# The depthwise convolution of a decoder layer on TensorE, with the shifted copies as the stationary operand

## What is computed

```python
def token_mixers(h, ctx_a, ctx_b, w_in, b_in, w_dw_a, b_dw_a, ln_conv_g, ln_conv_b, w_dw_b, w_o, b_o):
    z = h @ w_in + b_in                                    # (B, T, D_IN)
    a_val, a_gate, g_b, g_c, b_val = jnp.split(
        z, [D_A, 2 * D_A, 2 * D_A + D_B, 2 * D_A + 2 * D_B], axis=-1)
    # group A: Conformer conv module (GLU -> dwconv31 -> LN -> swish)
    u = a_val * jax.nn.sigmoid(a_gate)
    ua, new_ctx_a = causal_depthwise(ctx_a, u, w_dw_a)
    ua = jax.nn.silu(layer_norm(ua + b_dw_a, ln_conv_g, ln_conv_b))
    # group B: short gated conv  B * conv3(C * h)
    v = g_c * b_val
    vb, new_ctx_b = causal_depthwise(ctx_b, v, w_dw_b)
    ub = g_b * vb
    out = jnp.concatenate([ua, ub], axis=-1) @ w_o + b_o   # shared output projection
    return out, new_ctx_a, new_ctx_b

def trunk_layer(x, ...):
    x = layer_norm(ALPHA * x + 0.5 * swiglu(x, f1_wg, f1_wu, f1_wd), ln_f1_g, ln_f1_b)
    m, new_a, new_b = token_mixers(x, ctx_a, ctx_b, ...)
    x = layer_norm(ALPHA * x + m, ln_mix_g, ln_mix_b)
    x = layer_norm(ALPHA * x + 0.5 * swiglu(x, f2_wg, f2_wu, f2_wd), ln_f2_g, ln_f2_b)
```

## Time and profile before

| | us |
|---|---|
| median of 3 runs | 1200.44 (1195.74 to 1337.34) |
| the profiled execution | 1198.1 |
| its span, slowest core | 1196.4 |
| spans of the 8 cores | 1189.4 to 1196.4 |
| mean granted TensorE clock of the cores | 0.993 to 0.998 |
| TensorE busy | 1169.1 (98% of the span) |
| VectorE busy | 571.3 (48%) |
| ScalarE busy | 260.4 (22%) |
| GpSimd busy | 149.4 (12%) |

### The profile page before, as it was taken

One profiled execution on the slowest core, in us unless ns is written; L12 is line 12 of the kernel. 1 busy time (PEld: TensorE's weight loads), 2 busy tenths in 40 slices (PEclk: granted clock), 3 DMA queues, 4 the chain that ended last, 5 costly groups with the idle time before them and its releaser, 6 DMA issues.

```text
span 1196.4 us, 18592 instructions; the slowest of 8 cores (1189.4 to 1196.4 us)
## 1 busy us (share of the span) xinstructions
PE 1169.1 (98%) x6724; PEld 632.8 (53%) x6724; DVE 571.3 (48%) x874; ACT 260.4 (22%) x561; POOL 149.4 (12%) x212
## 2 busy tenths in 40 slices
PE   7999999999999999999999999999999999999997
PEld 5444444466666544455566544444444466666443
DVE  1122217742222387577888974557225532222475
ACT  1111110011111000349645432223100011111000
...
GB/s 157 134 152 174 176 107 150 115 120 177 77 71 73 45 126 137 139 128 119 128 162 164 138 157 140 157 128 108 197 107 121 88 147 80 74 71 36 36 126 88
DMA packets 78888, 144.43 MB, mean 121 GB/s; under 512 B 39872, under 2 KB 42304, under 8 KB 78784
## 3 DMA queue, kind: packets, MB, share of 16 engines
...
## 4 chain that ended last, share of the span: by engine, by line
PE 90%; DVE 5%; issue 2%; DMA 1%; ACT 1%; POOL 0%; DVEq 0%; SPq 0%; ACTq 0%; POOLq 0%
PE ps L591 59%; PE ps L575 28%; PE ps L860 1%; DMA sb_xT<-xpq 1%; PE ps L684 1%; DVE sb_xq L487 1%; DMA sb_xq<-xk 1%; DVE sb_stt L497 1%; DVE sb_RH L1022 0%; PE ps L878 0%; DVE sb_RW L954 0%; DVE sb_xq L521 0%; PE ps L561 0%; DVE sb_RW L933 0%; DVE sb_xq L491 0%
## 5 line engine op out<-in xcount | busy, mean ns | idle before, releaser
L591 PE MATMUL ps<-sb_xT,sb_ring 128*128 128x344 bf16 (+3 forms) x4384 | 770.1, 337 | 13.1 <-DMA sb_xT<-xpq 4.5
L591 PEld LDWEIGHTS ps<-sb_xT,sb_ring 128*128 128x128 bf16 x4384 | 428.3, 98 | 335.5 <-issue 17.9
L612 DVE TENSOR_TENSOR sb_RH<-sb_sg,ps 128x344 bf16<-128x344 f32 (+3 forms) x224 | 129.0, 576 | 453.6 <-ACT sb_sg L610 449.2
L575 PE MATMUL ps<-sb_RW,sb_RH 128*128 128x512 bf16 x1364 | 295.6, 379 | 0.6 <-DVE sb_xq L491 0.6
L610 ACT ACTIVATE sb_sg<-ps 128x344 f32<-128x344 f32 (+3 forms) x224 | 113.9, 508 | 618.5 <-PE ps L591 607.7
L575 PEld LDWEIGHTS ps<-sb_RW,sb_RH 128*128 128x128 bf16 x1364 | 133.2, 98 | 161.9 <-issue 1.9
L470 POOL TENSOR_TENSOR sb_mv<-sb_mv,sb_neghalf 128x1 f32<-128x1 f32 (+1 forms) x47 | 51.1, 1087 | 459.3 <-DVE sb_mv L468 459.3
L487 DVE SCALAR_TENSOR_TENSOR sb_xq<-sb_xq,ps 128x1024 f32<-128x1024 f32 (+1 forms) x50 | 60.8, 1217 | 88.2 <-PE ps L575 83.3
L406 POOL DMA_DIRECT2D sb_ring<-wgu x87 | 47.6, 548 | 410.0 <-PE ps L591 403.3
L528 DVE SCALAR_TENSOR_TENSOR sb_xq<-sb_xq,sb_mv,sb_lnb 128x1024 f32<-128x1024 f32 (+1 forms) x50 | 64.1, 1283 | 11.0 <-POOL sb_mv L470 6.2
L497 DVE BATCH_NORM_STATS2 sb_stt<-sb_xq 128x6 f32<-128x512 f32 (+1 forms) x100 | 64.1, 683 | 3.5
...
## 6 DMA issues: line engine op xcount, KB each, us to landing
...
```

What stands on the lines that cost most here:

```text
L575: ins = e.matmul(ps[:n, bank(yb + h)], lhsT=lhs(f), rhs=rhs(f, h), start=(f == 0), stop=(f == nk - 1))
L591: ins = e.matmul(out, lhsT=ring[:, slot, cw:cw + 128], rhs=xT_rhs(b, k, tok0, n), start=(k == 0), stop=(k == KC - 1))
L612: P.op("dve", lambda e: e.tensor_tensor(out=hT[:, f, tok0:tok0 + n], in0=sg[:, p_ % 2, :n], in1=ps[:, bu * 512: bu * 512 + n], op=ALU.mult ...
```

## The change

- **Convolution.** Stationary and moving operand change places: R2, shifted by 0 to 4 columns, is loaded, and the wide weights move. The result has tokens in the partitions at once. The biased copy, accP and the float32 transposes (`out`, `flip`) are gone; `put` reads the convolution's own bank one item later.
- **Bias.** Ahead of each group of five, one matmul with three rows adds the bias: `ones` (3 x 128) against `brow`, three bf16 rows whose sum is the float32 bias. `use_consts` makes them: a load into slot 4 of xq, five VectorE operations on one partition, three transfers.
- **Weights of the convolution.** They have four slots in place of three (the room of accP). The lists that say where they are made are new: in block 0 all eight by VectorE pieces.
- **Places and banks.** Block 0 convolves in banks 4 and 5, block 1 in 6 and 7. In block 1 the convolutions and the output projection's tiles stand at other items. The last gating item of block 0 goes to banks 4 and 5.
- **Turns.** For block 1, the TensorE turn stands ahead of the output projection's tile, and its ScalarE copy behind the item's `out`.
- **Chunks.** The second FFN's block 0 begins with three chunks on its first 512 tokens, not two (`u_items(0, 3)`).

```diff
@@ the constants @@
+            P.op("dve", lambda e: e.memset(ones[:], 1.0), writes=["ones"])
+            lo, hi = xq[0:1, 4, 0:DA], xq[0:1, 4, DA:2 * DA]
+            P.op("sp", lambda e: e.dma_start(out=lo, in_=bcd), writes=[("xq", 4)], dma="xq4")
+            P.op("dve", lambda e: e.tensor_copy(out=cs[0:1, 0, :], in_=lo), reads=[("xq", 4)], writes=[("cs", 0)])
+            for q, (a, r) in ((0, (lo, hi)), (1, (hi, lo))):
+                P.op("dve", lambda e, q=q, a=a, r=r: e.tensor_tensor(out=r, in0=a, in1=cs[0:1, q, :], op=ALU.subtract),
+                     reads=[("xq", 4), ("cs", q)], writes=[("xq", 4)])
+                P.op("dve", lambda e, q=q, r=r: e.tensor_copy(out=cs[0:1, q + 1, :], in_=r), reads=[("xq", 4)],
+                     writes=[("cs", q + 1)])
+            for q in range(3):
+                P.op("sp", lambda e, q=q: e.dma_start(out=brow[q:q + 1, :], in_=cs[0:1, q, :]), reads=[("cs", q)],
+                     writes=["brow"], dma="brow%d" % q)
@@ turn_pe: the copy is returned, and emitted by the caller @@
-            P.op("act", lambda e: e.activation(out=xT_tile(b, tok0, n),
+            return lambda: P.op("act", lambda e: e.activation(out=xT_tile(b, tok0, n),
@@ u_items @@
-        def u_items(b):
+        def u_items(b, ahead=2):
...
-            order = [(f, g) for g in gs for f in range(2)] + [(f, g) for f in range(2, NFC) for g in gs]
+            order = [(f, g) for g in gs for f in range(ahead)] + [(f, g) for f in range(ahead, NFC) for g in gs]
@@ conv @@
                     for g in range(4):
+                        c = i * 64 + g * 16
+                        ins = e.matmul(ps[:, bk * 512 + g * 128: bk * 512 + (g + 1) * 128].rearrange("p (k q) -> p k q", q=8),
+                                       lhsT=ones[:, :], rhs=brow[:, c:c + 16].unsqueeze(2).to_broadcast([3, 16, 8]),
+                                       start=True, stop=False)
                         for j in range(5):
                             a = (g * 5 + j) * 128
-                            ins = e.matmul(ps[:, bk * 512 + g * 128: bk * 512 + (g + 1) * 128], lhsT=wcs[ws][:, a:a + 128],
-                                           rhs=R2[:, sl, 4 * h + g, j:j + 128], start=(j == 0), stop=(j == 4))
+                            ins = e.matmul(ps[:, bk * 512 + g * 128: bk * 512 + (g + 1) * 128], lhsT=R2[:, sl, 4 * h + g, j:j + 128],
+                                           rhs=wcs[ws][:, a:a + 128], start=False, stop=(j == 4))
@@ spread_s3, block 1 @@
-                    ev.append(((m + lag, 0), 1, lambda i=i: trn(i, tb[i % len(tb)])))
+                    ev.append(((m + lag, 0), -1, lambda i=i: cp.update({i: trn(i, tb[i % len(tb)])})))
+                    ev.append((m + lag, 0, lambda i=i: cp[i]()))
@@ the mixer of block 0 @@
-                    [(4, 5), (6, 7), (8, 9), (11, 12), (12, 13), (13, 14), (14, 15, 15, 16), (16, 16, 17, 17)],
-                    (4, 5), (6, 7))
-        spread(sides, [18, 19, 20, 21, 20, 21, 22, 23], conv_w(2)[0] + conv_w(0)[0])
+                    [(4, 5), (5, 6), (7, 7), (8, 9), (11, 12), (12, 13), (14, 14), (15, 16)], (4, 5))
+        spread(sides, [16, 17, 18, 19, 18, 19, 20, 21, 20, 21, 22, 23], conv_w(0)[0] + conv_w(1)[0] + conv_w(2)[0])
+        spread(sides, [21], [lambda: state.update(other=True)])
@@ the mixer of block 1 @@
-        spread(sides, [2, 5, 8, 11], conv_w(1)[0])
-        spread_s3(sides, 0, [10, 12, 14, 16, 19, 22, 24, 27], (4,), (7,), 6, 3)
+        spread(sides, [2, 5, 8, 11], conv_w(3)[0])
+        spread_s3(sides, 0, [10, 12, 14, 16, 19, 21, 23, 27], (4,), (7,), 6, 3)
-        spread_conv(sides, [15, 16, 18, 21, 23, 26, 28, 31],
-                    [None, None, None, range(16, 20), (19, 20), range(20, 24), (23, 24), range(25, 29)], (6,), (7,))
+        spread_conv(sides, [15, 16, 18, 20, 22, 24, 26, 28],
+                    [None] * 4 + [range(16, 20), (19, 20), range(20, 24), range(24, 28)], (6, 7))
@@ the second FFN, block 0 @@
-        run(u_items(0), sides)
+        run(u_items(0, 3), sides)
```

63 lines of the change are left out of this document (23 added, 40 removed).

## The result

The changed kernel is a little slower, where I had forecast a little faster. In nine runs each, taken in turn on one chip, its median was 1206.21 us and that of the kernel before 1199.39 us. The ratio is 1.007, with a 95% interval from 1.0052 to 1.0089, so the loss is about 8 us. The ratio is taken over the fast executions alone; the medians are of all nine, with the slow ones in which a die ran at a lower clock. The loss lies within 2%, but the time is above the range that the prediction gave (to 1206.0), and the sign is the other one. The interval is 0.4% wide, so this measurement tells much smaller differences than the 2% of which the prediction said that it is about what can be told.

The account below looks back on a forecast made before the run. TensorE was taken to bound the kernel, busy 1169.1 of 1196.4 us. From 1198.1 us, terms -7.0, -1.2, +6.0, +0.4, -3.9, +1.0, -4.6, -1.8 and +5.4 gave 1192.4 us; range 1183 to 1206 us.

Parts of the forecast that it names:

- transposes and their waits gone: Convolution: 64 float32 transposes leave TensorE, -7.0 us, and the waits they met go too, -1.2 us.
- 64 bias matmuls: Convolution: one three-row matmul ahead of each group of five, +6.0 us, bounds 3.1 to 9.3 us.
- start of block 1: Mixer: the 1.11 us bank wait reappears two items later; +0.4 us, bounds 1.1 gained to 0.4 lost.
- wait near item 27 gone: Second half of block 1: the 2.27 us bank-space wait and its slow clock go, -3.9 us, other end 0.
- new short waits in block 1: Second half of block 1: new short waits from a denser schedule, +1.0 us.
- turns: Second FFN: the new order removes a 2.94 us TensorE wait and its slow stretch, -4.6 us, at worst 0.
- three ahead: transposed input: After block 1: the 2.35 us wait for the last tile of xT shrinks to 0.6, -1.8 us; other end +3.3.
- three ahead: late fetch of chunk 4: Second FFN, item 8: TensorE waits 3.7 us for chunk 4, plus 1.7 us of slow clock, +5.4 us.
- the shifted operand might load slowly: Rival, convolution: shifted stationary operands load at 110 ns against 56.5, +17.1 us, giving 1209.5 us; chance 0.12.
- transfers starve TensorE: Rival, second FFN: chunk 2 takes 13.4 us and chunk 4 9.5 us or more, about 1201 us; chance 0.13.
- my own three marks of an error: Wrong if a run of 24 exceeds 2 us, item 8's wait is missing, or block 1 has new VectorE waits.
- the third or the fourth rival: Transfers starving TensorE, about 1201 us, chance 0.13; or re-placed work making its own waits, 1201 us, chance 0.10.

Follow-up runs that it names:

- e2: The changed kernel without the 64 bias matmuls (bias left out of the computation); ratio 1.0001 to the kernel before.
- e4: The changed kernel with the bias multiplied as 128 rows, 125 of them zero; ratio 1.0018 to the kernel before.
- e14: The changed kernel with the bias multiplied as 64 rows, 61 of them zero; one time of 1205.8 us.
- e6b_ahead3: The kernel before with only three chunks ahead in the last input block instead of two; ratio 1.0058 to the kernel before, +6.9 us.
- e7_best3: The changed kernel with the bias as 128 rows, three chunks ahead and next chunks asked for at every item; ratio 0.9955 to the kernel before.
- e10_oldlists: The changed kernel with the placing tables of the kernel before in blocks 0 and 1; ratio 1.0114 to the kernel before.
- e1_ahead2: The changed kernel with two chunks ahead in the second FFN again; ratio 1.0026 to the kernel before.
- e3: The changed kernel without the bias matmuls and with no shift of the stationary operand; a single time of 1196.7 us.

## Why the prediction was wrong, point by point

The terms against what the two traces show, in us:

| step of the prediction | forecast | measured |
|---|---|---|
| transposes and their waits gone | -8.2 | -8.2 (none is left) |
| 64 bias matmuls | +6.0 (3.1 to 9.3) | +16.7 |
| start of block 1 | +0.4 | +1.1 |
| wait near item 27 gone | -3.9 | -3.9 |
| new short waits in block 1 | +1.0 | +2.1 to 2.5 |
| turns | -4.6 | -4.6; alone -6.6 in time |
| three ahead: transposed input | -1.8 | -2.35 |
| three ahead: late fetch of chunk 4 | +5.4 | +7.9 |

**The step that failed is the price of a bias matmul,** and the bounds that I put on it. The run of 24 grew by 1.05 us (16 times, 16.7 us), of which I had 6.0, with 9.3 as the highest: 10.7 of the 14.1 us that are missing. I had used a row with four short transposes, seen a start 0.09 us late, and charged it once. The change is paid twice, into the short matmul and out of it, 0.10 us each, on top of 56 ns. Going out was not visible in my row, because I read only where the next start stood and not whether the load behind it had its usual lead. I also discounted the upper bound as "one case", to a value in the middle; the measured price was 1.8 times the upper bound. My lower bound came of the same slip: the 48 ns were the mean of four starts with the way out in it. Read with their loads, the rows gave the price before any run: 0.09 us in, some 0.09 out and the 56 ns of a full matmul make about 0.24 us. e2, e4 and e14 show the price from three sides. With 16.7 in place of 6.0 the sum gives 1203.1 us, a loss of 5.0, so this one term also turned the sign.

The Trainium skill (TensorE: Matmul & The Clock Gate, LDWEIGHTS) is right that a load of few rows takes as long as a full one (0.09 us against 0.10 in the rows above). The price that follows from the 81 ns which the Trainium skill gives on the same page (Back-to-back issue gap), 5.2 us for the 64, is a third of the 16.7 us measured.

**The late fetch** was foreseen at its place, with its cause, and sized too small. I had 3.7 us of waiting and 1.7 of slow clock; it was 5.04 and 2.9. The fetch took 7.9 us, where my rows said 5.4 to 7.2. On the four cores that finished first the wait was 3.06 to 3.49 us and the clock's part 1.3 to 1.7, close to what I had; on the other four it was longer, and the slowest core sets the time. e6b_ahead3 and e7_best3 confirm the mechanism: the wait appears without the rest of the change and goes when the fetch is asked for earlier.

**The start of block 1** went as the prediction says, the wait at a later item behind VectorE's first multiplication; its waits add up to 3.6 us against 2.5 before, 0.7 more than I took. **New short waits** were 1 to 1.5 us more, at the last items, where I had not looked at the order of LayerNorm and gating on VectorE. Less the half microsecond by which the transposed input did better, these terms make 14.4 to 14.9 us against the 14.1 missing, which is within what executions differ by.

**Right were** the turns, 2.94 + 1.68 us in the trace and alone -6.6 us (4.7 to 8.5, so 4.6 lies at the edge); and the vanished wait near item 27, a part of which e10_oldlists brings back. The term of the transposed input came out too, but not by the edit alone. In the kernel before that wait stood on the two slowest cores (2.35 and 3.66 us), with 0.33 us or none on the other six; after the change none has it, and e1_ahead2 has 1.9 us of it again. In e6b_ahead3, with the same edit and the old places, chunk 2 was late instead. That the shifted operand might load slowly, which had 0.12, is excluded by e2 and e3. That transfers starve TensorE, which had 0.13, did not happen in this kernel, where chunk 2 landed in 8.0 us and the only late one was asked for late; its first half did happen in e6b_ahead3 (14.3 us). Of my own three marks of an error two came true: a run of 24 takes over 2 us, and a new wait on VectorE stands in block 1.

**The range** did not fail by the one term: with the measured price of the bias and all else as forecast the sum is 1203.1 us, inside it, and with 7.9 us for the fetch 1205.6, still inside. The start of block 1 and the new short waits, 1.8 to 2.2 us together, carried it over. To the high end I had let the third or the fourth rival lift it, never a bias price above 146 ns.
